# Four edits of a two-block kernel: start of the first norm, condition products in a norm, a norm split by streams, and half products in the last scan

## What is computed

```python
h = layer_norm(x, ln_in_g, ln_in_b)
for i in range(2):
    proj = h @ w_in[i] + b_in[i]
    conv_out = conformer_conv(a, g, ...)             # 31 taps, 512 channels
    attn_out = neighbourhood_attention(...)          # 8 heads
    h = layer_norm(ALPHA * h + concat([conv_out, attn_out]) @ w_out[i] + b_out[i], ...)
    f = swiglu(h, ...) if i == 0 else moe_swiglu(h, ...)    # dense, then 8 experts
    h = layer_norm(ALPHA * h + f + sigmoid(h @ ple_gate_w[i] + ...) * (p[i] @ ple_w[i]), ...)
# second block: x = h, and a context of 256 more tokens
for l in range(2):
    shift, scale, gate = split(silu(c) @ w_ada[l] + b_ada[l])     # for x, and for the context
    xn = rmsnorm(x, g) * (1 + scale_x) + shift_x ;  cn = rmsnorm(ctx, g) * (1 + scale_c) + shift_c
    q, k, v, ... = xn @ w_in, cn @ w_in              # attention, and a gated scan over chunks of 128
    x = x + gate_x * (concat([att_x, m_x]) @ w_out)  # in layer 0 the context too
return rmsnorm(x, final_g)
```

## Time and profile before

| what | value |
|---|---|
| median of three runs | 2178.56 us (2178.12 to 2184.68) |
| the profiled execution's own time | 2172.15 us |
| its span, first to last instruction | 2170.3 us |
| PE busy (matmul records) | 2047.5 us, 94% |
| DVE, ACT, POOL busy | 776.0, 404.2, 5.8 us |
| mean granted TensorE clock | 0.988 |
| bytes moved, mean rate | 506.73 MB, 233 GB/s |
| PE on the chain that ended last | 88% |

### The profile page before, as it was taken

How to read it: one execution, slowest core, us unless ns; L and a number is a source line. 1 busy time by engine, 2 the same in 40 slices (tenths; PEclk the granted TensorE clock), 3 DMA queues, 4 the chain that set the end, 5 groups by cost and what they waited for, 6 DMA issues and landing times.

```text
span 2170.3 us, 36820 instructions
## 1 busy us (share of the span) xinstructions
PE 2047.5 (94%) x15880; PEld 1485.3 (68%) x15880; DVE 776.0 (36%) x1750; ACT 404.2 (19%) x958; POOL 5.8 (0%) x12
## 2 busy tenths in 40 slices
PE   7999999899989999999999999998999989899877
PEld 5869999886866666666666656666645666476766
DVE  5836555585231111111011110114156364335454
ACT  1133110104220111000100000002133432123221
POOL 0000000000000000000000000000000000000000
PEclk9999999999999999999999999999999999999998
DMA  8483445346089999999999999993211111232100
GB/s 304 156 295 128 164 157 193 117 153 242 32 332 375 420 418 416 420 420 420 420 419 421 420 420 419 417 417 137 97 59 40 39 40 43 74 117 78 59 20 20
DMA packets 71939, 506.73 MB, mean 233 GB/s; under 512 B 7776, under 2 KB 9824, under 8 KB 11232
## 3 DMA queue, kind: packets, MB, share of 16 engines
q1 hardware_dynamic: 69296, 497.18, 57.5%
q0 software_dynamic: 1152, 4.19, 0.8%
q10 hardware_dynamic: 1328, 2.97, 0.4%
HBM read 503.27 MB, written 1.05 MB: 232 GB/s over the span
## 4 chain that ended last, share of the span: by engine, by line
PE 88%; DMA 5%; DVE 4%; ACT 2%; issue 1%; SPq 0%; DVEq 0%; ACTq 0%
PE ps L449 86%; DMA work<-weights 3%; DMA ring<-weights 1%; PE ps L1114 1%; PE ps L690 1%; DVE work L2527 0%; DMA par<-params 0%; PE ps L566 0%; DVE work L1885 0%; ACT work L1707 0%; DVE work L2484 0%; DVE work L2488 0%; DVE work L2485 0%; DVE work L2594 0%; PE ps L1215 0%
## 5 line engine op out<-in xcount | busy, mean ns | idle before, releaser
L449 PE MATMUL ps<-work 128*32 128x256 f32 (+8 forms) x5608 | 588.9, 383 | 30.7 <-DVE work L2527 11.3
L449 PE MATMUL ps<-work,ring 128*128 128x256 f32 (+2 forms) x2056 | 521.3, 409 | 12.0 <-DVE work L2409 6.0
L449 PEld LDWEIGHTS ps<-work 128*32 128x32 f32 (+3 forms) x5608 | 380.0, 138 | 195.5 <-issue 122.7
L449 PE MATMUL ps<-ring,work 128*32 128x256 f32 (+3 forms) x4824 | 468.7, 410 | 11.9 <-ACT work L1431 3.2
L449 PEld LDWEIGHTS ps<-work,ring 128*128 128x128 f32 x2056 | 355.4, 193 | 148.9 <-issue 113.2
L449 PEld LDWEIGHTS ps<-ring,work 128*32 128x32 f32 (+1 forms) x4824 | 260.1, 120 | 147.1 <-issue 75.7
L449 PE MATMUL ps<-xc,ring 128*128 128x256 f32 (+1 forms) x1440 | 277.7, 354 | 11.1 <-DVE xc L1901 7.1
L449 PEld LDWEIGHTS ps<-xc,ring 128*128 128x128 f32 x1440 | 244.7, 193 | 45.6 <-issue 12.1
L2147 DVE TENSOR_TENSOR work<-work,ps 128x256 f32<-128x256 f32 x42 | 17.7, 421 | 418.3 <-ACT work L1564 418.3
L449 PE MATMUL ps<-xc,work 128*128 128x256 f32 (+1 forms) x720 | 138.3, 351 | 1.4 <-DMA work<-weights 1.4
L449 PEld LDWEIGHTS ps<-xc,work 128*128 128x128 f32 x720 | 120.9, 191 | 21.3 <-DMA work<-weights 4.9
(11 more groups left out here) (266 smaller groups left out, 1163.0 us busy)
## 6 DMA issues: line engine op xcount, KB each, us to landing
ring<-weights SPq DMA_DIRECT2D x317, 1024.0 KB, 11.9
work<-weights SPq DMA_DIRECT2D x154, 1024.0 KB, 16.1
work<-rel POOLq DMA_DIRECT2D x8, 512.0 KB, 11.4
con<-consts ACTq DMA_DIRECT2D x1, 1368.0 KB, 9.9
xc<-x_t SPq DMA_DIRECT2D x1, 1024.0 KB, 7.5
xc<-ctx_t ACTq DMA_DIRECT2D x1, 1024.0 KB, 21.5
out<-work SPq DMA_DIRECT2D x1, 1024.0 KB, 3.9
par<-params SPq DMA_DIRECT2D x1, 872.0 KB, 9.4
```

Source lines behind the costliest of these rows:

```text
L449: ins = eng.matmul(o, lhs, rhs, start=start, stop=stop, **kw)
```

## The change

It makes four edits.

1. Start: the three first loads have a semaphore each. PE waits for the constants, runs two 512-column matmuls whose result nobody reads (`spin(2)`), then waits for `x_t` alone and starts the norm; after the norm three more (`spin(3)`). DVE waits for the parameters inside the norm, after centring. ACT makes the condition's input after the norm. The three late loads go from ACT's queue to SP's, behind the first six units.
2. Condition: the first four of the 12 units of layer 1 (`ADA_EARLY`) are made in the norm behind the dense network, two rows ahead of its mean, two turns between mean and variance, two rows and two turns after the variance. Layer 1's `conditions` has 9 steps in place of 13. The four units stand in that place in the order of the weights.
3. Norm between the layers of block 2: `rms1` is over the 256 columns of the stream; the context's variance (`context_var`), root, reciprocal and products come behind it, on PE, ACT and DVE. ACT's squares stay over 512 columns. Only the key tile, the first that reads the context, waits for it.
4. Output pieces: the attention half of output chunks 4 to 7 of layer 1 is computed as four more pieces in the scan (20 pieces for 16), each closed in bank 7, which ACT copies, times the gate, to `xc[:, c, T:2T]`; DVE adds these to `xc` at the start of `block2_out`. At the end only the scan half of these chunks is left. The last layer's output units come in the order chunks 4 to 7, then 0 to 3.

The diff, cut:

```diff
+            def spin(n):
+
+                for _ in range(n):
+                    mm(ps[:, 7, :], ones, con[:, 0:512], True, True)
...
+            def context_var():
+
+                o = fill(("ctx_var1",), 2, (s["ctx_std"], 2))
+                b = squares("rms1", False)
+                for c in range(KC):
+                    last = mm(o[:, 0:T], ones, b[:, c, T:2 * T], c == 0, c == KC - 1)
+                last.then_inc(bank_full[2], 1)
...
-                    if fresh[0].startswith("rms"):
-                        eng.wait_ge(s["norm_out_a"], KC * int(fresh[0][-1]) + c + 1)
+                    if fresh[0] == "rms0":
+                        eng.wait_ge(s["norm_out_a"], c + 1)
...
+            def condition_row(l, u, bank):
+                w = next_unit()
+                o = fill(("row", l, u), bank, (s["cond_row"], UNITS_ADA * l + u + 1))
+                for c in range(KC):
+                    at = 32 * (c % 4)
+                    last = mm(o[at:at + 32, 0:GW], cond_s[:, c, :], w[:, c * GW:(c + 1) * GW], c < 4, c >= KC - 4)
+                last.then_inc(bank_full[bank], 1)
+
+            def condition_turn(l, u, mod_t):
+                eng.wait_ge(s["cond_row"], UNITS_ADA * l + u + 1)
+                for half in range(2):
+                    at = 2 * (2 * u + half)
+                    last = mm(mod_t[:, at:at + 2], cond_row[:, u % 2, half * P:half * P + P],
+                              con[:, CN("fold", 0, 2)], True, True)
+                return last
...
-                mod_t = fill(("mod", l), 0, (s["mod_out"], l + 1))
-                for u in range(UNITS_ADA + 1):
+                mod_t = fill(("mod", l), 0, (s["mod_out"], 2 * l + 1))
+                for u in range(l * ADA_EARLY, UNITS_ADA + 1):
...
+            def norm_beside_conditions():
+
+                condition_row(1, 0, 7)
+                condition_row(1, 1, 4)
+                norm_mean("ln2_0", res, KC, T)
+                mod_t = fill(("mod_early",), 5, (s["mod_out"], 2))
+                condition_turn(1, 0, mod_t)
+                condition_turn(1, 1, mod_t)
+                norm_var("ln2_0", KC, T, True)
+                condition_row(1, 2, 7)
+                condition_row(1, 3, 4)
+                condition_turn(1, 2, mod_t)
+                condition_turn(1, 3, mod_t).then_inc(bank_full[5], 1)
...
+                    if l and n > T:
+                        eng.wait_ge(s["norm_out_a"], KC * l + k + 1)
...
+                if l == 1:
+                    eng.wait_ge(s["att_out"], CC * (l + 1))
+                    for c in range(CC, KC):
+                        if c % 2 == 0:
+                            late_units.append(next_unit(beside=c > CC))
+                        o = fill(("xh", c), 7, (s["xo_half"], c - CC + 1))
+                        out_half(l, late_units[-1], c, o, 0).then_inc(bank_full[7], 1)
+                        finished["xh", c] = now[0]
+                        yield
...
-                total = (32 if l == 0 else 16) - SCAN_START[l]
+                total = (32 if l == 0 else 20) - SCAN_START[l]
...
+                alone = l == 1 and c >= CC
                 n = 2 * T if l == 0 else T
                 for k in range(CC * half, CC * half + CC):
                     last = mm(o[:, 0:n], w[:, k * GW + (c % 2) * P:k * GW + (c % 2) * P + P], mix2[k][:, 0:n],
-                              k == 0, k == KC - 1)
+                              k % (CC if alone else KC) == 0, (k + 1) % (CC if alone else KC) == 0)
...
-                        w = next_unit()
-                        if c == 2:
+                        w = next_unit(beside=l == 1)
...
+                    if l:
+                        w = late_units[c // 2 - 2]
+                    elif c % 2 == 0:
                         w = next_unit()
                     o = fill(("xo", l, c), c, (s["x_added"], KC * l + c + 1))
-                    out_half(l, w, c, o, 0)
+                    if l == 0:
+                        out_half(l, w, c, o, 0)
...
-            eng.wait_ge(s["inputs_loaded"], 16 * N_INPUTS)
+            eng.wait_ge(s["ones_loaded"], 16)
+            spin(2)
+            eng.wait_ge(s["x_loaded"], 16)
             norm("in", xc, KC, T)
+            spin(3)
...
-                    norm("ln2_0", res, KC, T)
+                    norm_beside_conditions()
...
-                    norm("rms1", xc, KC, 2 * T, centred=False)
+                    norm("rms1", xc, KC, T, centred=False)
+                    context_var()
...
+                if n == SLOTS - 1:
+                    eng.dma_start(con[:, CN.early:], consts[:, CN.early:]).then_inc(s["late_loaded"], 16)
+                    eng.dma_start(p_sb, p_t).then_inc(s["late_loaded"], 16)
+                    eng.dma_start(xc[:, :, T:2 * T], ctx_t).then_inc(s["late_loaded"], 16)
...
+                if l == 1:
+                    for c in range(CC, KC):
+                        yield "xh", c
+                        o = tile(eng, "xh", c)
+                        eng.activation(xc[:, c, T:2 * T], o[:, 0:T], ACT.Copy, scale=mod[:, l, 2 * KC + c, 0:1])\
+                            .then_inc(s["xo_half"], 1)
...
-            eng.wait_ge(s["inputs_loaded"], 16 * N_INPUTS)
-            eng.dma_start(con[:, CN.early:], consts[:, CN.early:]).then_inc(s["late_loaded"], 16)
-            eng.dma_start(p_sb, p_t).then_inc(s["late_loaded"], 16)
-            eng.dma_start(xc[:, :, T:2 * T], ctx_t).then_inc(s["late_loaded"], 16)
+            eng.wait_ge(s["ones_loaded"], 16)
+            norm("in", KC, T)
+            eng.wait_ge(s["params_loaded"], 16)
...
+                    condition_row(1, 0)
+                    condition_row(1, 1)
                     norm("ln2_0", KC, T)
+                    condition_row(1, 2)
+                    condition_row(1, 3)
...
-                    norm("rms1", KC, 2 * T, centred=False, src=xc)
+                    norm_squares("rms1", KC, 2 * T, centred=False, src=xc)
+                    norm_std("rms1", KC, T, centred=False)
+                    v = tile(eng, "ctx_var1")
+                    eng.activation(std2[:, T:2 * T], v[:, 0:T], ACT.Sqrt, bias=con[:, CN("eps6")], scale=1.0 / D)\
+                        .then_inc(s["ctx_std"], 1)
...
+            def context_scaled_last():
+                eng.wait_ge(s["ctx_std"], 2)
+                link(eng.reciprocal(rstd2[:, T:2 * T], std2[:, T:2 * T]))
+                for c in range(KC):
+                    eng.tensor_tensor(xn[:, c, 1, :], xc[:, c, T:2 * T], rstd2[:, T:2 * T], ALU.mult)\
+                        .then_inc(s["ctx_scaled"], 1)
...
+                if l == 1:
+                    for c in range(CC, KC):
+                        eng.wait_ge(s["xo_half"], c - CC + 1)
+                        eng.tensor_tensor(xc[:, c, 0:T], xc[:, c, 0:T], xc[:, c, T:2 * T], ALU.add)\
+                            .then_inc(s["x_half"], 1)
                 for c in range(KC):
                     o = tile(eng, "xo", l, c)
+                    if l == 1 and c == CC:
+                        eng.wait_ge(s["x_half"], KC - CC)
...
+            eng.wait_ge(s["x_loaded"], 16)
+            norm("in", xc, KC, T, layer_gain("ln_in_g", "ln_in_b", xc), beside=prepare)
...
```

93 lines of the change are left out of this document (46 added, 47 removed).

## The result

The changed kernel takes 2167.02 us (median of 11 runs, 2150.24 to 2176.55); the kernel before, run beside it, 2181.89 us (11 runs, 2178.00 to 2187.09). The medians are 14.9 us apart where 25.2 were forecast. The ratio, which is taken over all runs and not from the two medians, is 0.9913, with a 95% interval of 0.9892 to 0.9933: that is 19 us, and between 15 and 24. The time forecast, 2153.4 us, is 13.6 us too low, and the range (2144 to 2166) ends 1 us under the median; of this, 3.3 us are the kernel before itself, which took 2181.89 here and 2178.56 in the three runs that the forecast started from. Set against 2178.56, the ratio gives 2159.6 us, inside the range.

A forecast was written before the change was run, and what follows sets the result against it. TensorE holds 88% of the last chain; the expert stage, bound by PE and DMA at once, stays unchanged. Gains of 4.5 + 6.8 + 7.45 + 6.45 = 25.2 us take the median from 2178.56 to 2153.4 us, range 2144 to 2166.

The forecast's parts named there:

- nearer the cold end: Start: the mean ends between 12.1 (clock risen at once) and 15.5 us (not at all); 14.3 taken, 1.2 us more gain.
- upper end: Layer 1's attention: gain 4.7 us, range 4.0 to 6.3, where 6.3 is all PE time of four rows and turns.
- The 1.6 us of this term: Norm between block 2's layers: share of the 7.45 us gain said to hang on the clock, for the first tiles.
- with the work denser: Last scan: the clock, at 0.56 before, may not fall; between 0 and 3.7 us of gain, 1.4 taken.
- I count it in full: Expert stage: its loads wait for the routing behind block 1, so an earlier start is kept as gain in full.
- The caution that was weighed against the rows: All clock terms: by the skill page slow matmuls should not be fitted; without the clock's part the sum would be 18 us.
- 7.2 us of clock terms: Parts hanging on the clock: start 1.2 and 0.7, condition 1.9 and 0.35, split norm 1.6, scan 1.4.
- (a): Filled idle places: the clock falls all the same, lower ends hold; 13.6 us gain, 2165.0 us; chance 0.14.
- (e): Last scan: the four pieces fall on its path in full, 6.9 us, edit 4 gives nothing; 2160 us; chance 0.09.
- (b): Whole kernel: clock holds everywhere, attention loses its rows in full; upper ends, 32 us gain, 2146.5 us; chance 0.12.
- (c): Expert stage: gives the head start back, edits 1 and 2 count nothing; 13.9 us left, 2164.7 us; chance 0.04.
- (d): Expert stage: its stream runs slower from the new start; at 400 GB/s it costs 34 us, 2188 us; chance 0.03.

The follow-up runs named there:

- early table: Changed kernel with idle matmuls in block 1's attentions and the last scan, plus ACT squaring one unread column before its first norm; median 2149.83 us, ratio 0.9846.
- edit 3 alone: Only the split norm between block 2's layers, made on the kernel before; median 2179.56 us, ratio 0.9993.
- scan's clock held: Changed kernel with idle matmuls in block 1's attentions and also in the last scan, ahead of state changes, turn and last product; median 2151.28 us, ratio 0.9854.
- edit 4 alone: Only the four added output pieces in the last scan, made on the kernel before; median 2176.91 us, ratio 0.9968.

## Why the forecast was right in its signs and places and wrong in its size

The forecast's terms stand against one pair of traces above. Fourteen traces show most of its stretches, and they repeat closely where the clock does. Left out are kernels that add or take away idle matmuls in the stretch or load the table early:

| stretch | without the edit, us (traces) | with it, us (traces) | gain | in the pair | forecast |
|---|---|---|---|---|---|
| edit 1: to the first gate sigmoid | 32.68 to 35.69, mean 33.86 (5) | 30.89 to 32.85, mean 31.90 (5) | 2.0 | 4.80 | 4.5 |
| edit 2: mean behind the dense network to the sigmoid behind it | 22.22 to 22.95, mean 22.57 (5) | 20.48 to 21.38, mean 20.77 (9) | 1.8 | 2.08 | 2.1 |
| edit 2: from there to the output projection, clock at 1.00 | 107.45, 107.47 (2) | 102.87, 102.88 (2) | 4.6 | 4.58 | 4.7 |
| edit 3: sum of squares to the last scan | 161.58 to 161.81 (5) | 154.21 to 154.23 (9) | 7.4 | 7.59 | 7.45 |
| edit 4: last scan to the final sum | 117.33 to 117.36 (4), 121.49 (1) | 113.36 to 114.62, mean 114.21 (7) | 3.1 | 2.78 | 6.45 |

The gains add up to 18.9 us, which is what the ratio (19) and the means (18.1) show. So two terms were sized wrong, that of edit 1 by 2.5 us and that of edit 4 by 3.3.

**Edit 1 (4.5; 4.80 in the pair, 2.0 over ten traces).** The trace that the forecast was read from was one in which the parameters came late. PE waits for them until 11.34 us there, and until 11.88, 10.22, 9.80 and 9.04 in the four other traces with the old start, of which this is the earliest:

```profile
9.04 6.26 PE L452 MATMUL ps<-xc,con 128*128 128x256 f32 x16 [9.04 <-DMA par<-params]
```

In the nine traces with the new start the first sum starts at 8.66 us in the mean. So the wait that falls away is 1.8 us in the mean and not 2.6. In the pair itself x landed at 8.95, not 8.7, and the mean ended at 12.67, 1.6 us sooner than the 14.3 taken: the choice "nearer the cold end" was wrong for this execution and right for two of the six with these idle matmuls. Against it stands a cost that the sum did not have. The forecast put "ACT's Silu with its two table loads" behind the norm and found cover for both; it overlooked that in its old place the Silu had brought the table with which the squares run too, under the mean:

```profile
12.88 1.28 ACT L1820 ACT_TABLE_LOAD   x1 [12.72 <-issue]
14.18 0.22 ACT L1820 ACTIVATE work<-par 128x16 f32<-128x16 f32 x1
18.68 2.74 ACT L1420 ACTIVATE work<-work 128x256 f32<-128x256 f32 x8 [4.29 <-DVE work L1876]
```

This is ACT in the kernel before: no load between the Silu and the squares. With the Silu moved, the squares need a load of their own (13.30 in the changed kernel), and PE waits for it: idle 2.39 for 1.05. Two errors that nearly cancel, and parameters that came late, gave a good sum: that 4.80 agrees with 4.5 is luck. The early table takes the cost of the load away (1.34 us).

**Edit 2 (6.8; 2.07 + 4.58).** Right in both terms, and repeated. The rows fill the idle time, the mean takes 3.69 us for the 3.45 taken, and the projection starts with the clock at its upper level. The attention loses what PE's rows and turns had held, and the chain of DVE and ACT behind it came within 0.1 us of the working. (Four rows and turns of 1.54 us are 6.2 us, not the 6.3 of its upper end.)

**Edit 3 (7.45; 7.59).** Right, and repeated. Idle near 0 before the first product and no wait of the key tile for ACT: its eight modulations run from 1879.19 to 1883.23, 5 us before the copy at 1888.24. The 1.6 us of this term that the forecast counts as the clock's are not worked out there.

**Edit 4 (6.45; 2.78 in the pair, 3.1 over twelve traces).** This is the step that failed by most, in one term: "the clock stood at 0.56, which cost 2.75 us on the path; with the work denser it may not fall ... I take 1.4". The 6.9 us at the end came in full (64 records for 96). The start of the output product's attention half moved from 83.19 us behind the scan's start (2037.76 to 2120.95) to 87.22 (2019.89 to 2107.11, behind the last piece), 4.03 us later, where 1.85 less 1.4 had been forecast. How much of this is the clock's can be estimated from the rows: at the three places of the changed kernel the records take some 7.1 us more than the same records do at the upper clock (3.62 for 1.89, 2.06 for 1.13, and so on), at the two of before some 4.3. That is 2.8 us more, and 1.2 are left for the placement of the pieces, worked out as 1.85. So the clock did not stay up, it fell at one more place, and the term is about -2.8 and not +1.4. It was no chance of this execution: the seven traces of kernels with the pieces lie within 1.3 us of each other. Only one of the five without them shows a third place too (edit 3 alone, 121.49 us). That there was a gain to be had by the clock in this stretch is shown by the kernel with the scan's clock held, 7.4 us faster, of which 1.7 come from the last product (13.92 us from its start to the final sum, for 15.60). The reason given for a gain, "with the work denser", was the error: a piece in a gap of 3.5 us moves the gap, and the idle times of 1.6 to 3.6 us between DVE and PE stayed.

**The expert stage (0; -1.1).** "I count it in full" holds. From its first products to the one behind it the stage takes 880.43 us in the trace of before, 881.55 in the changed kernel's, and 881.35 to 883.34 in the twelve others, those with the entry of the kernel before among them (edit 3 alone 881.35, edit 4 alone 881.86). The trace of before was the quickest of fourteen, and the loss in the pair is no effect of the edits.

**From the trace to the median.** The forecast takes the gain between two traces for that between two medians: the median "goes to 2178.56 - 25.2". The profiled execution of before, at 0.988, was a rare one: two of 87 later executions had as much. The median stands at 0.981, and the changed kernel's, 0.982 to 0.983, not at the 0.990 of its trace. What the medians carry on top are the falls in block 1's attention, which come and go: in the traces one fall costs 6 to 12.5 us. Here both traces were lucky by about as much, so that their difference (20.7 us) lies inside the interval of the ratio (15 to 24 us), and this step explains little of the miss; with one lucky trace it would have been off by 13 us. The caution that was weighed against the rows (the Trainium skill's page "TensorE: Matmul & The Clock Gate", section "What's actually happening": the number of slow matmuls differs from run to run and should not be fitted) would have given 18 us. That is close to the 18.1 and 19 that were measured, but not for its reason alone: of the 7.2 us of clock terms it would have dropped those of edits 2 and 3 too, which came in (the mean of edit 2's norm takes 3.69 us for 5.38 in every trace that has the edit), and kept the 2.6 of edit 1, of which 1.8 came in and the table load took 1.3.

**The rivals.** (a) forecast 13.6 us and 2165.0, 2 us from the median, but not by its mechanism: the clock was held where edits 1, 2 and 3 filled idle places (the rows above), and fell only in edit 4's. (Its sum takes 5.0 for edit 4, whose lower end was given as 4; with 4 it is 12.6.) Its gain is under what the ratio's interval allows (15 to 24 us). (e), pieces on the scan's path in full, is wrong: four pieces of 1.73 us came in for 4.0 us, more than half of that the clock's by the estimate above. (b) is out by the scan, (c) and (d) by the expert stage, which starts sooner and takes as long as in the other traces.

## What to carry to other kernels

Where a kernel's time has steps in it, set the mean granted clock of each execution beside its time before anything else: here one straight line (2 us for each thousandth) turned four results, two of which could not be told from nothing, into four sizes that add up. It leaves out what an edit gives by way of the clock, so the plain ratio has to stand beside it. A profile is one execution: take each stretch from several traces before a term is built on it, above all a wait for a DMA (the parameters came anywhere from 9.04 to 11.88 us) and a place where the clock may fall. Where PE's own work is made of small matmuls or broken by short waits, idle matmuls put into the waits bought 15.8 us in two places, nearly what the four edits gave together, and the times then repeated to within 5 to 10 us.

## What was not expected of the hardware

- The granted clock stood at 0.50, which is 1.2 GHz, for over 20 us of block 1's attention, with a record on PE throughout: rows with 32 columns of weights, turns with 2 columns, scores over 64 rows. It did so in some executions of a kernel and not in others. What sets it off was not found. The four traces with idle matmuls ahead of it have no fall, seven of the ten without have one or two.
- In the first windows, up to some 18 us, the granted clock shows 1.00 though the sum runs at half rate: this row of the kernel before is a sum at 0.42 us for a record, and the clock column gives no sign of it. That the slow sum is the clock's is inferred: the same sum takes 3.72 us in four of six traces with idle matmuls ahead of it. At the start the durations are to be read, not the column.

```profile
11.34:18.10 6.76, 6.76 (x16) 1.00 1.01 423
```

- The same kernel gave medians of 2181.09 and 2169.78 in two sets of nine runs, 11 us apart, with ratios of 0.9976 and 0.9939. That is as much as two of the edits are worth together.
